# Expert slots handled one by one, products cut into pieces, and three token tiles merged and routed before the slots begin

## The reference

```python
q = (hb @ w_pq).reshape(t, P_HEADS, 2, P_QDIM // 2)
sc = jnp.einsum('thpd,hpkd->thpk', q, keys)          # 8 heads, 2 halves, 128 keys
sv, si = lax.top_k(sc, P_TOPK)                       # 16 of 128, twice per head
cand = (sv[:, :, 0, :, None] + sv[:, :, 1, None, :]) # 16 x 16 sums per head
cv, ci = lax.top_k(cand, P_TOPK)                     # 16 experts per head, of 16384
eidx = jnp.take_along_axis(cidx, ci, axis=-1)
gate = jax.nn.softmax(cv, axis=-1)
act = gelu(einsum('thkd,td->thk', u_tab[eidx], hb))
out = einsum('thk,thkd->td', gate * act, v_tab[eidx])
```

## Time and profile before

| | |
|---|---|
| median of 3 runs | 7569.1 us (7564.6 to 7570.45) |
| profiled execution, its own time | 7554.87 us |
| its span | 7553.1 us |
| mean granted TensorE clock | 0.762 of full |
| busy: PE, DVE, ACT, POOL | 58%, 41%, 19%, 20% |
| HBM read | 1566.56 MB, of it 1342.26 MB by the gathers |
| slots | 1280, L682 |

### The profile page before, as it was taken

How to read it: one execution, slowest core, us unless ns; L and a number is a source line. 1 busy time by engine, 2 the same in 40 slices (tenths; PEclk the granted TensorE clock), 3 DMA queues, 4 the chain that set the end, 5 groups by cost and what they waited for, 6 DMA issues and landing times.

```text
span 7553.1 us, 59355 instructions
## 1 busy us (share of the span) xinstructions
PE 4377.6 (58%) x18966; PEld 1902.7 (25%) x18966; DVE 3105.2 (41%) x7579; ACT 1460.9 (19%) x4806; POOL 1477.2 (20%) x1454
## 2 busy tenths in 40 slices
PE   7999726555553256355579996366545523454455
PEld 2576412222221011111135854022212200111111
DVE  1531462223334354645445215522233344555454
ACT  0142011111111122222222421111111111222222
POOL 0200011111111123234322000111111111333333
PEclk9999857877775577767789998677877756766777
DMA  5102335554554489799941023355555445888998
GB/s 191 55 13 85 133 132 198 201 208 181 191 193 165 178 317 384 282 366 358 363 160 55 1 112 130 142 200 205 202 189 186 182 151 204 327 339 308 361 359 326
DMA packets 222742, 1573.73 MB, mean 208 GB/s; under 512 B 25648, under 2 KB 27312, under 8 KB 35040
## 3 DMA queue, kind: packets, MB, share of 16 engines
q0 software_dynamic: 184320, 1342.26, 47.0%
q1 hardware_dynamic: 38112, 227.68, 8.0%
HBM read 1566.56 MB, written 3.28 MB: 208 GB/s over the span
## 4 chain that ended last, share of the span: by engine, by line
PE 37%; DMA 33%; DVE 14%; ACT 6%; issue 6%; POOL 2%; DVEq 1%; ACTq 0%; SPq 0%; POOLq 0%
DMA arena<-in_experts,arena 31%; PE ps L920 16%; PE ps L704 8%; DVE sq L1374 7%; ACT arena L1061 3%; PE ps L825 2%; ACT arena L1054 2%; PE ps L848 2%; POOL arena L682 2%; DMA arena<-in_weights 2%; PE ps L721 2%; PE ps L870 1%; PE ps L838 1%; PE ps L894 1%; ACT arena L1050 1%
## 5 line engine op out<-in xcount | busy, mean ns | idle before, releaser
L920 PE MATMUL ps<-arena 64*64 64x512 f32 x10240 | 1974.6, 902 | 2843.9 <-ACT arena L1061 2842.5
L1374 DVE CUSTOM_DVE_ANT_0 sq<-arena 128x1024 f32<-128x1024 f32 x1280 | 1568.6, 1225 | 2904.2 <-DMA arena<-in_experts,arena 2875.6
L682 POOL DMA_INDIRECT arena<-in_experts,arena x1280 | 1341.2, 1048 | 5500.4 <-PE ps L920 4283.4
L920 PEld LDWEIGHTS ps<-arena 64*64 64x64 f32 x10240 | 516.4, 186 | 4146.4 <-issue 4145.0
L1050 ACT ACTIVATE arena<-arena 128x2 f32<-128x2 f32 x640 | 130.2, 203 | 4670.5 <-DVE arena L1374 4670.5
L704 PE MATMUL ps<-arena 128*128 128x512 f32 (+3 forms) x1920 | 776.6, 561 | 25.7 <-DMA arena<-in_weights 23.8
L704 PEld LDWEIGHTS ps<-arena 128*128 128x128 f32 x1920 | 369.1, 195 | 432.1 <-issue 383.5
L1054 ACT ACTIVATE arena<-arena 128x1 f32<-128x1 f32 x1280 | 425.5, 379 | 46.3 <-issue 2.4
L1061 ACT ACTIVATE arena<-ident,arena 128x128 f32<-128x128 f32 x1280 | 433.3, 385 | 0.0
L894 PE MATMUL ps<-arena 128*128 128x256 f32 (+1 forms) x1024 | 321.1, 471 | 79.3 <-ACT arena L1026 62.0
L1267 DVE TENSOR_REDUCE negm<-ps 128x1 f32<-128x768 f32 (+4 forms) x160 | 119.0, 745 | 381.2 <-PE ps L831 214.8
(11 more groups left out here) (148 smaller groups left out, 3182.0 us busy)
## 6 DMA issues: line engine op xcount, KB each, us to landing
arena<-in_weights SPq DMA_DIRECT2D x182, 1024.0 KB, 6.8
arena<-in_experts,arena POOLq DMA_INDIRECT x1280, 7.9
arena<-mod_rows SPq DMA_DIRECT2D x24, 512.0 KB, 8.7
arena<-in_weights SPq DMA_DIRECT2D x8, 576.0 KB, 4.7
arena<-in_weights SPq DMA_DIRECT2D x4, 768.0 KB, 4.8
arena<-in_weights SPq DMA_DIRECT2D x6, 512.0 KB, 4.7
x<-in_x_sample SPq DMA_DIRECT2D x4, 512.0 KB, 11.3
arena<-in_g_norm SPq DMA_DIRECT2D x4, 512.0 KB, 11.0
```

What stands on the lines that cost most here:

```text
L682: pool.indirect_dma_start(out=ring[BUF[n]], out_offset=None, in_=ins["experts"], in_offset=bass.IndirectOffsetOnAxis(ap=index[n // SLOTS % ...
L920: last = MM(acc[h][to:to + 64, c * 512:(c + 1) * 512], diag[(n + odd) % 4][lo:lo + 64, lo:lo + 64], ring[BUF[n + odd]][lo:lo + 64, D + c * ...
L1374: V.tensor_tensor_reduce(out=sq[:], in0=ring[BUF[n]][:, 0:D], in1=h2_of_slot(n), scale=1.0, scalar=0.0, op0=ALU.mult, op1=ALU.add, accum_o ...
```

## The change

It does six things. (1) Every item of the slot pipeline is for one slot: `E` is one dot, `Ea` is Gelu, the product with the gate and the diagonal, all on ACT, and `Emm` adds one slot. DVE's two small operations per pair go; the gate is no longer halved. (2) `g`, `o`, `pq` are cut into four pieces and `p` into two, `tk2` into six, `tk1` into one per tile; a new class `Line` sorts them among the slots at even distances: slot n has its dot at n, its activation at n + 0.4 and its product at n + 1.6. (3) Group 0 is now tiles 0, 1 and 2, before the slots; group 1 is tiles 3 and 4, beneath slots 16 to 232. (4) For the tiles after tile 0, the four Exp and divisions become one of each. (5) The ring has 5 buffers for the first 20 slots, 6 up to slot 260 and 9 after it; buffer 4 of it is the place of gains, masks and rotary rows, so those are loaded anew at the end of layer 0, and `consts` of layer 1 moves behind all slots of layer 0. (6) The `choose` and `mod` items move: tile 1 beneath slots 20 to 110, tile 2 beneath 232 to 250, tile 3 beneath 262 to 330, `mod` beneath 300 to 560, tile 4 beneath 390 to 460.

```diff
-def turn(l, t, u):
-    return [("tk2", l, t, u), ("tkx", l, t, u), ("tkg", l, t, u)]
+def turn(l, t, u, alone):
+    s = [("tk2", l, t, u, j) for j in range(6)]
+    return s + ([("tkx", l, t, u), ("tkg", l, t, u)] if alone else [])
...
-            s += [("sc", l, gid, q - 1), ("tk1", l, gid, q - 1)]
+            s += [("sc", l, gid, q - 1)] + [("tk1", l, gid, q - 1, j) for j in range(len(GROUPS[gid]))]
...
-GROUPS = {0: (0, 1), 1: (2, 3, 4)}
+GROUPS = {0: (0, 1, 2), 1: (3, 4)}
...
+def pieces(items):
+    s = []
+    for i in items:
+        n = {"g": 4, "o": 4, "p": 2, "pq": 4}.get(i[0], 1)
+        s += [("part", i, j, n) for j in range(n - 1)] + [i]
+    return s
...
+class Line:
+    def spread(self, a, b, items):
+        total = sum(cost(i) for i in items)
+        at = 0.0
+        for i in items:
+            at += cost(i)
+            self.points.append((a + (b - a) * at / total, i))
+
+    def slots(self, l):
+        n = l * NT * SLOTS
+        for s in range(NT * SLOTS):
+            self.put(s, [("E", n + s)])
+            self.put(s + .4, [("Ea", n + s)])
+            self.put(s + LAG, [("Emm", n + s)])
...
+LAG = 1.6
...
-        s.stretch(r[at:], 6)
-        s.stretch(choose(l, 1) + merge(l, 1) + route(l, 1), 2 * NGRP - SEAM - 12 - 6)
-        s.stretch(choose(l, 2), 12)
-        s.stretch([], SEAM + 2)
-        s.stretch(choose(l, 3), 16)
-        beneath = [("consts", 1)] + mod_items(1) if l == 0 else []
-        s.stretch(beneath, NGRP - 16)
-        s.stretch(choose(l, 4), 16)
-        s.stretch([], 2 * NGRP - 18)
-        s.flush()
+        line.spread(-2, 16, pieces(r[at:]))
+        line.spread(20, 110, choose(l, 1))
+        line.spread(16, 232, pieces(merge(l, 1) + route(l, 1)))
+        line.spread(232, 250, choose(l, 2))
+        line.spread(262, 330, choose(l, 3))
+        if l == 0:
+            line.spread(300, 560, mod_items(1))
+        line.spread(390, 460, choose(l, 4))
+        s += line.items()
+        if l == 0:
+            s += [("consts", 1)]
...
-NBUF = 8
+NBUF = 9
...
+for _l in range(L):
+    BUF += [s % 5 for s in range(20)]
+    BUF += [s % 6 for s in range(236)]
+    BUF += [(s + 2) % 6 for s in range(4)]
+    BUF += [(s + 6) % 9 for s in range(380)]
...
                 elif kind == "consts":
                     if l:
-                        sp.wait_ge(*ready("oT", 0, NT - 1, 1))
-                        sp.wait_ge(*ready("qcN", 0, NT - 1))
-                        sp.wait_ge(ob_ready, NT)
-                    sp.dma_start(gains[:], to_all(row("gains", l))).then_inc(consts_in, 16)
+                        sp.wait_ge(slot_used, FINAL_IN[0, 4] + 1)
+                        sp.dma_start(mask, ins["mask"]).then_inc(masks_in, 16)
+                        sp.dma_start(rope, ins["rope"]).then_inc(masks_in, 16)
+                    sp.dma_start(gains, to_all(row("gains", l))).then_inc(consts_in, 16)
...
                 elif kind == "Emm":
-                    for odd in range(2):
-                        pe.wait_ge(row_land[BUF[n + odd]], 16 * TURN_OF[n + odd])
-                    pe.wait_ge(diag_done, n + 2)
+                    pe.wait_ge(row_land[BUF[n]], 16 * TURN_OF[n])
+                    pe.wait_ge(diag_done, n + 1)
                     for c in range(2):
-                        for odd in range(2):
-                            for h in range(2):
-                                lo, to = 64 * h, 64 * (h ^ odd)
...
-                    last.then_inc(slot_used, 2)
+                        for h in range(2):
+                            lo, to = 64 * h, 64 * (h ^ (n % 2))
+                            last = MM(acc[h][to:to + 64, c * 512:(c + 1) * 512], diag[n % 4][lo:lo + 64, lo:lo + 64],
+                                      ring[BUF[n]][lo:lo + 64, D + c * 512:D + (c + 1) * 512], start=s < 2, stop=s >= SLOTS - 2)
+                    last.then_inc(slot_used, 1)
...
-                elif kind == "E":
-                    n = GRP * item[1]
-                    c = n % 8
-                    act.wait_ge(dot_done, n + GRP)
-                    A(dsq[:, c:c + GRP], dots[:, c:c + GRP], ACT.Square, scale=(GELU_A * GELU_B) ** 0.5)
-                    A(dlin[:, c:c + GRP], dots[:, c:c + GRP], ACT.Copy, scale=GELU_A)
+                elif kind == "Ea":
+                    n = item[1]
+                    c, s = n % 16, n % SLOTS
+                    act.wait_ge(dot_done, n + 1)
+                    A(gel[:, c:c + 1], dots[:, c:c + 1], ACT.Gelu_apprx_tanh)
                     act.drain()
-                    for s in range(c, c + GRP):
-                        last = A(dth[:, s:s + 1], dsq[:, s:s + 1], ACT.Tanh, scale=dots[:, s:s + 1], bias=dlin[:, s:s + 1])
...
+                    A(wts[:, c:c + 1], gel[:, c:c + 1], ACT.Copy, scale=gate[n // SLOTS % 2][:, s:s + 1])
+                    act.drain()
+                    if n >= 4:
+                        act.wait_ge(slot_used, n - 3)
+                    A(diag[n % 4], ident[:], ACT.Copy, scale=wts[:, c:c + 1]).then_inc(diag_done, 1)
```

More of the change, by code:

```diff
@@ L181, in mod_items @@
     return s
-GRP = 2
-NGRP = SLOTS // GRP
 ETILES = [(l, t) for l in range(L) for t in range(NT)]
-def tensor_cost(item):
-    k = item[0]
[L192 to L197, removed]
-    def __init__(self):
[L202 to L252, removed]
@@ L256, with cost @@
-SEAM = 6
+def pieces(items):
[4 more added lines that the diff above has]
+    return s
+def cost(item):
+    k = item[0]
+    if k == "part":
+        k, n = item[1][0], len(GROUPS[item[1][2]]) if item[1][0] == "pq" else 1
+    else:
+        n = len(GROUPS[item[2]]) if k in ("pq", "sc") else 1
+    return {"mod": 7.0, "hT2": 1.2, "g": 1.76, "p": 1.76, "mT": 1.2, "o": 1.76, "pq": .5 * n, "sc": .25 * n,
+            "n2": 3.0, "tk2": 1.5, "tk1": 1.0}.get(k, 0.1)
@@ new lines, with put, items @@
+class Line:
+    def __init__(self):
+        self.points = []
+    def put(self, at, items):
+        self.points += [(at, i) for i in items]
+    def spread(self, a, b, items):
[10 more added lines that the diff above has]
+            self.put(s + LAG, [("Emm", n + s)])
+        for t in range(NT):
+            end = (t + 1) * SLOTS - 1 + LAG
+            self.put(end + .1, [("ea", l, t), ("ex", l, t)])
+            after = [("sw", l, t, 0), ("sw", l, t, 1), ("ew", l, t)] + ([("g2", l, 1)] if t == 0 else []) + ([("y", t)] if l == L - 1 else [])
+            self.put(end + 2.1, after)
+    def items(self):
+        return [i for _, i in sorted(self.points, key=lambda p: p[0])]
@@ L375 @@
 for _it in ITEMS:
+    if _it[0] == "part":
+        _it = _it[1]
     for _b in blocks_of(_it):
@@ L495, in build @@
         top_i = lambda t: zt(t)[:, 1280:1536].bitcast(U32)
-        ring = [at(2048 * r, 2048) for r in range(4)] + [ar(HT0, 2048), ar(HT0 + 2048, 2048), at(8192, 2048), at(10240, 2048)]
+        ring = [at(2048 * r, 2048) for r in range(4)] + [front[:, 0:2048], ar(HT0, 2048), ar(HT0 + 2048, 2048), at(8192, 2048), at(10240, 2048)]
         tmpk = [sq[:, 256 * r:256 * (r + 1)] for r in range(2)]
@@ L510, in build @@
         esum = take(8)
-        dots, dsq, dlin, dth, dgate, wts = (take(8) for _ in range(6))
+        dots, gel, wts = (take(16) for _ in range(3))
         assert _e[0] <= R0 + 22928
@@ L699, in weight, with project @@
                 return block_in(b)
-            def project(dst, lhs, blocks, cols):
-                for k in range(DK):
+            def project(dst, lhs, blocks, cols, steps):
+                for k in steps:
                     w = weight(blocks[k // 4]).rearrange("p (k n) -> p k n", k=4)
@@ L708, in _ @@
             for item in ITEMS:
+                if item[0] == "part":
+                    _, item, piece, count = item
+                else:
+                    count = {"g": 4, "o": 4, "p": 2, "pq": 4}.get(item[0], 1) if (("part", item, 0, 2) in PLACE or ("part", item, 0, 4) in PLACE) else 1
+                    piece = count - 1
                 kind = item[0]
@@ L711, in _ @@
                 if item in BANK:
-                    for before in BEFORE[item]:
-                        pe.wait_ge(*ready(*before))
+                    if piece == 0:
+                        for before in BEFORE[item]:
+                            pe.wait_ge(*ready(*before))
                     dst = psum(item)
-                done = lambda op: op.then_inc(full_sem[kind], 1)
+                done = lambda op: op.then_inc(full_sem[kind], 1) if piece == count - 1 else op
+                steps = lambda n: range(piece * n // count, (piece + 1) * n // count)
                 blocks = blocks_of(item)
@@ L868, in _ @@
                     w = weight(blocks[0]).rearrange("p (k n) -> p k n", k=4)
-                    for k in range(4):
+                    for k in steps(4):
                         last = MM(dst, oT(t)[:, 4 * (bc // 2) + k, :], w[:, k, :], start=k == 0, stop=k == 3)
@@ L880, in _ @@
                     pe.wait_ge(*ready("mT", l, t))
-                    for k in range(DK):
```

(10 more changed lines are left out.)

154 lines of the change are left out of this document (80 added, 74 removed).

## The result

The kernel after takes 5646.4 us (median of three runs, 5644.06 to 5646.91) against 7569.1: a ratio of 0.746, 95% interval 0.7443 to 0.7477. The forecast was 6230 with a range of 5950 to 6700: the direction was right, the size too small by 584 us.

A forecast was written before the change was run, and what follows sets the result against it. The prediction saw some 240 slots per layer waiting for a loop of latencies at 5 buffers in pairs, the rest bound by DMA. Stage sums of 3195 and 3021 gave a span of 6216, so 6230 us; range 5950 to 6700.

The forecast's parts named there:

- The DMA term: Late slots, stages d and e: gathers bound by DMA at 2.92 us per slot, 200 us and 905 us without `mod`.
- term for `mod`: Stage e of layer 0: 25.2 MB of `mod` weights at 370 GB/s add 68 us to 905, giving 973.
- Stage b: Slots 16 to 232, two tiles beneath: PE the bound, DMA close behind, 807 us, 3.74 us per slot.
- a quarter of the work at 1.2 GHz: PE in slots 16 to 232: part of its work at low clock, taking 645 us at full clock to 807.
- (3): Rival: PE holds 2.4 GHz throughout, stage b is DMA's 704 us, median 5975 us; chance 0.13 with anything better.
- (1): Rival: PE stays at 1.2 GHz, slots don't overlap, 3.69 us per slot everywhere, 7794 us; chance 0.04 together with (4).
- (2): Rival: coupling of in-order queues eats the gain beneath, stage b at 5.0 us per slot, median 6775 us; chance 0.18.
- (4): Rival: slots beneath stay at 6.24 us, something else than the ring sets them; about 7750 us; chance 0.04 with (1).
- the third tile: Before the first gather: merging a third tile bare adds 92 us on PE, all on the path; first slot at 975.
- the seam's constants: Between layers: masks, rows and gains loaded after slot 636, mostly hidden; 4 us, bounds 0 and 20.
- stage c: Slots 232 to 262: four turns and 18 dots on DVE 71 us, then 12 slots at 2.92: 106 us.
- Stage a: Slots 0 to 16, rest of `route` with tile 0's turns: bound by DVE, 112 us times 1.2, 134 us.

The follow-up runs named there:

- b_front: Kernel before, pairs kept, one ring buffer more in layer 1 only (6 instead of 5, then 9 instead of 8): 6944.7 us, 0.9188.
- early5: Kernel after with 5 ring buffers instead of 6 for slots 20 to 260: 5725.7 us, 0.7565.
- pair_add: Kernel after, but PE adds an even slot right before the odd one after it; dots and activations stay single: 5591.0 us, 0.7397.
- four_exp: Kernel after with Exp and division once per turn for every tile, as before, instead of once per tile: 5661.2 us, 0.7487.
- pair4: Kernel after with pair_add's list, but PE adds two slots as one item in the old order, both buffers freed at its end: 5663.6 us, 0.7486.

## Why the prediction was wrong in size

By stages, forecast against measured, layer 0 and layer 1:

| stage | forecast | measured |
|---|---|---|
| start to first gather | 975 / 869 | 972 / 862 |
| a, slots 0 to 16 | 134 / 134 | 119 / 119 |
| b, to 232 | 807 / 807 | 684 / 683 |
| c, to 262 | 106 / 106 | 102 / 101 |
| d, to 330 | 200 / 200 | 173 / 170 |
| e, to 640 | 973 / 905 | 827 / 777, and 23 / 32 to the end |

**The DMA term was mis-sized; it is 276 of the 571 us between the sums** (d and e: 27 + 146 - 23 and 30 + 128 - 32). The step that failed is "With 8 buffers the gathers fill the DMA engines", 2.86 us each, on which I put 2.92 for every late slot and bounds of 2.75 and 3.0. Measured were 2.49 to 2.55. I took a busy share of 0.93 for a ceiling. b_front shows that it wasn't: one more buffer and nothing else in this stage took it from 937.7 to 826.8 us. A hint stood in my own term for `mod`: plain loads on top of the gathers had run at 370 GB/s, more than the gathers alone at 353. The sign "the bare end of a layer unchanged at 2.9 us per slot" failed with it.

**Stage b, 247 us of it.** Its mechanism was right: single slots and the sixth buffer end the loop of latencies (early5, b_front), and PE becomes the busiest with DMA close behind; a slot of 8 records takes 1.93 us where I put 1.95, and PE was busy 616 us where I had 645 at full clock, as neighbours already overlap here and there. Wrong was the step "I put a quarter of the work at 1.2 GHz": the granted clock was 0.97. Had I left the quarter out, PE's 645 would have stood below my own DMA term of 704, and with DMA at 2.49 that is 613; the stage took 684. So neither bounds it alone: whole products (+41), five buffers instead of six (+36) and neighbours added together on PE (-13) each move it a little. The remaining 48 us between the sums lie in stages a and c and in the two starts.

**The rivals.** (3), full clock throughout, was nearest: clock 0.97 in stage b and 0.98 in the late slots, though 0.84 in stage a and 0.81 in c. The Trainium skill (TensorE: Matmul & The Clock Gate, "HAM oscillation") says the same of loops without long PE gaps; by that rule, the trace agrees. Its 5975 is still too high, mainly since it kept my DMA rate. (1), low clock, is refuted by the same 0.98 in the late slots. (2), coupling at 5 us per slot, did not come: stage b took 3.17 us per slot. (4), slots beneath at 6.24 us as before, is refuted by the same number.

**Right:** 92 us for the third tile (972.1 against 882.5, 90), the seam's constants (I took 4 us; DVE's norm sums start 1.8 us after the start of the last add, before it was 1.4), stage c (102 against 106), 20 us of table loads per layer hidden (two layers 38.5). Stage a was near, 119 against 134, but not for my reason alone: DVE is busy 81.5 us of it where I had summed 112, and pair_add, which changes only PE's order, takes it to 106.

For Tanh I had bounds of 0 and 24 loads; it is 0. The Trainium skill (ScalarE: Activation LUTs, "What ACT_TABLE_LOAD costs") gives 2.66 us for a switch to another set, load and drain. The load itself is 1.283 us here as there; what the whole pays in four_exp is 0.3 us for each of the 48 more loads in the mean. By its windows it is at most 0.8 in slots 16 to 262 (9.5 us for 12 loads) and under 0.1 in the late slots with 9 buffers, so the slack of the ring covers nearly all there and part of it before.

**Where the 1923 us come from,** as far as edits alone show it. One buffer more, in pairs, is 610 us in one layer. In the changed kernel the sixth early buffer is worth 79, buffers 7 to 9 late 26, the pieces 87, the third bare tile 64, one Exp per tile 15. These don't add up to the whole, and can't: ring and single handling cure the same lack, free buffers. In slots 16 to 232 of one layer the sixth early buffer brings 400 us to pairs (b_front) and 36 to 45 to single slots (early5). How much single handling alone would bring to the kernel before was not run.

## What to carry to other kernels

In a ring of buffers, count those that are ahead, not those that exist: pairs that wait for their successors held four of five, and one buffer more brought 610 us in one of two layers, two thirds of it in the stage with 5 buffers. Take a DMA share of 0.95 for a ceiling only when the rate no longer moves with one more transfer in flight. Whether to move work beneath a stage depends on what bounds it: the same tile was 120 us per layer worse bare while the ring was the bound, 32 better once PE was full, and worse again once neighbours overlapped on PE; so the fastest version here, 5466 us, 3.2% below the kernel after, keeps single slots, pieces and ring, puts neighbours next to each other on PE and goes back to two tiles bare.

## What the runs showed of the hardware

- Gathers of 8 KB rows, with the `mod` loads among them, ran at 420 GB/s over the 827 us of stage e, 2.49 us per gather at best, with 9 buffers, at 412 with 6 and at 388 with 5. In pairs it was 347 with 8 and 394 with 9 (layer 1, no `mod`). Packet time filled 0.90 to 0.97 of the engines at 347 to 394 GB/s too.
- Two float32 slots of 8 records in complementary quadrants took 1.96 us together and 1.93 each alone (pair_add), without being interleaved in the program.
- The same work, placed more densely, came with a lower granted clock. The rows are of late slots of layer 0, 201 us long in both kernels. The kernel after, one slot at a time, has PE 158 us busy at 0.99 (window of its last 80 slots):

```profile
2677.10:2878.00 200.90, 158.18 (x648) 45.85 (x648) 98.00 (x159) 70.44 (x236) 77.82 (x80) 0.99 1.01 421
```

  pair4, both slots in four quadrants at once, has it 118 us busy at 0.78:

```profile
2691.20:2892.40 201.20, 117.61 (x656) 30.42 (x652) 97.89 (x159) 70.90 (x237) 91.51 (x80) 0.78 1.01 421
```
